# Low parts of the gate and up weights written over their raw chunks, with the next load waiting for the multiplication

## The reference, cut to what matters

```python
fn = rms_norm(h, g_ffn_pre[i])
ff = (jax.nn.silu(fn @ w_ffn_gate[i]) * (fn @ w_ffn_up[i])) @ w_ffn_down[i]
h = h + rms_norm(ff, g_ffn_post[i])
```

```python
c_act = jax.nn.silu(c)
mod = jnp.dot(c_act, w_ada[l]) + b_ada[l]
```

## Time and profile before

| | |
|---|---|
| median of 3 runs | 3594.81 us (3594.74 to 3598.14) |
| the profiled execution's own time | 3603.56 us |
| its span, first to last instruction | 3602.0 us |
| TensorE matmuls, busy | 3317.0 us, 92% of the span |
| VectorE busy | 1967.7 us, 55% |
| ScalarE busy | 1221.4 us, 34% |
| gate and up stage | about 540.7 to 1044.4 us |
| down stage | about 1044.4 to 1284 us |

### The profile page before, as it was taken

The page is one execution under the profiler, slowest core; times in us unless marked ns, Lnnn a source line. Parts: engine busy times, 40 slices in busy tenths (PEclk is TensorE's granted clock), DMA queues, the critical chain, the costliest instruction groups (busy, mean ns, idle before and its releaser), DMA issues.

```text
span 3602.0 us, 42919 instructions
## 1 busy us (share of the span) xinstructions
PE 3317.0 (92%) x15906; PEld 2611.5 (73%) x15906; DVE 1967.7 (55%) x2283; ACT 1221.4 (34%) x1263; POOL 823.4 (23%) x535
## 2 busy tenths in 40 slices
PE   7998779999999979789877799999999899999996
PEld 6874338888888844434556799888888688888885
DVE  4233457788865535550256579555555455555555
ACT  1122024444434420100242333455555343443431
POOL 2000000000000000000001478887888600100010
PEclk9999889999999989889988899999999899999998
DMA  7433547777755566579224256666666666666663
GB/s 257 141 123 111 187 152 272 273 278 279 277 191 191 198 234 247 219 273 358 75 84 163 94 179 178 211 216 214 210 212 216 181 248 235 244 240 242 238 246 116
DMA packets 194539, 747.53 MB, mean 208 GB/s; under 512 B 53873, under 2 KB 53905, under 8 KB 124321
## 3 DMA queue, kind: packets, MB, share of 16 engines
q1 hardware_dynamic: 129696, 664.84, 51.8%
q0 software_dynamic: 55552, 64.91, 6.7%
q10 hardware_dynamic: 9216, 16.78, 1.3%
HBM read 710.62 MB, written 35.83 MB: 207 GB/s over the span
## 4 chain that ended last, share of the span: by engine, by line
PE 69%; POOL 16%; DVE 8%; issue 4%; DMA 2%; ACT 2%; POOLq 0%; ACTq 0%; DVEq 0%; SPq 0%
POOL weight_dram L2107 15%; PE bank L435 15%; PE bank L581 10%; PE bank L582 10%; PE bank L583 10%; PE bank L587 9%; PE bank L419 7%; PE bank L588 5%; DMA weight_dram<-misc 1%; PE bank L372 1%; PE bank L850 1%; PE bank L484 1%; DVE aux L1916 0%; POOL part_lo L2087 0%; DMA misc<-in_w_ada 0%
## 5 line engine op out<-in xcount | busy, mean ns | idle before, releaser
L1880 DVE TENSOR_TENSOR part_lo<-ring,part_hi 128x2048 fp32r<-128x2048 f32 x248 | 568.0, 2293 | 406.5 <-ACT part_hi L1343 386.9
L1343 ACT ACTIVATE part_hi<-ring 128x2048 fp32r<-128x2048 f32 x252 | 482.8, 1916 | 550.9 <-PE bank L583 293.9
L2107 POOL DMA_INDIRECT weight_dram<-misc x256 | 571.1, 2231 | 101.6 <-issue 95.2
L587 PE MATMUL bank<-h_both,part_hi 128*128 128x512 f32 x1664 | 579.6, 392 | 8.1 <-DVE part_lo L1880 8.1
L435 PE MATMUL bank<-ring,xT 128*128 128x512 f32 (+1 forms) x1216 | 510.7, 581 | 8.0 <-DVE xT L1543 6.3
L587 PE MATMUL bank<-h_both,ffn_hi 128*128 128x512 f32 x1408 | 493.7, 397 | 4.8 <-DVE ffn_lo L1643 4.8
L588 PE MATMUL bank<-h_both,part_lo 128*128 128x256 f32 x1664 | 467.1, 281 | 0.0
L435 PEld LDWEIGHTS bank<-ring,xT 128*128 128x128 f32 x1216 | 226.9, 192 | 291.7 <-issue 289.9
L581 PE MATMUL bank<-part_hi,coef_hi 128*128 128x512 f32 x1024 | 399.7, 390 | 17.6 <-DVE part_lo L1880 17.6
L582 PE MATMUL bank<-part_lo,coef_hi 128*128 128x512 f32 x1024 | 399.4, 390 | 0.0
L583 PE MATMUL bank<-part_hi,coef_lo 128*128 128x512 f32 x1024 | 399.3, 390 | 0.0
(11 more groups left out here) (315 smaller groups left out, 4415.4 us busy)
## 6 DMA issues: line engine op xcount, KB each, us to landing
ring<-in_u_table SPq DMA_DIRECT2D x128, 1024.0 KB, 4.9
ring<-in_v_table SPq DMA_DIRECT2D x128, 1024.0 KB, 4.8
ring<-in_stream SPq DMA_DIRECT2D x114, 1024.0 KB, 6.3
misc<-in_w_ada SPq DMA_DIRECT2D x192, 512.0 KB, 5.7
ring<-in_gateup SPq DMA_DIRECT2D x88, 1024.0 KB, 4.9
ring<-in_down SPq DMA_DIRECT2D x44, 1024.0 KB, 4.8
ring<-in_wo_pq SPq DMA_DIRECT2D x32, 1024.0 KB, 4.8
weight_dram<-conv_tmp POOLq DMA_DIRECT2D x1, 16384.0 KB
```

The source lines that it names most:

```text
L587: nc.tensor.matmul(out[:, 0:2 * S], hi, x_pair, start=start, stop=False)
L1343: a.activation(part_hi[j % PARTS], raw[j % RAW], ACT.Copy).then_inc(sem("hi_ready"), 1)
L1880: v.tensor_tensor(part_lo[j % PARTS], raw[j % RAW], part_hi[j % PARTS].bitcast(F32), ALU.subtract).then_inc(sem("lo_ready"), 1)
L2107: g_.indirect_dma_start(out=places, out_offset=bass.IndirectOffsetOnAxis(ap=gstage[:, t, k:k + 1], axis=0), in_=wstage[:, t, k:k + 1], in_ ...
```

## The change: what it does

The low part of a gate or up chunk is written over the raw chunk (`down_lo`, four places), and the two places in `nat` are no longer used. VectorE's subtraction needs no wait for TensorE any more, and it is done one chunk earlier in VectorE's order (c + 3 in place of c + 2), so three are done ahead of the first round. The place of a raw chunk is now free only when TensorE has multiplied it, so SyncE's wait ahead of the chunk four later is on `multiplied`, and so is the wait of the first four chunks of down.

```diff
@@ -220,7 +220,6 @@
 
         ffn_raw = [ring[:, i * CH:(i + 1) * CH] for i in range(RAW)]
         ffn_hi = [rounded(f"ffn_hi{i}", "ring", (RAW + i) * CH, CH)[:, :] for i in range(PARTS)]
-        ffn_lo = [rounded(f"ffn_lo{i}", "nat", i * CH, CH)[:, :] for i in range(2)]
         down_lo = [rounded(f"down_lo{i}", "ring", i * CH, CH)[:, :] for i in range(RAW)]
         hid_parts = [rounded(f"hid_parts{i}", "misc", i * 8 * S, 8 * S)[:, :].rearrange("p (a k s) -> p a k s", a=2, k=4)
                      for i in range(2)]
@@ -708,7 +707,7 @@
                 for j in range(8):
                     if j < loads:
 
-                        sp_.wait_ge(sem("lo_ready"), j + 1 + 8 * it)
+                        sp_.wait_ge(multiplied, PLAN["gateup"]["chunk"] + j + 1 + 8 * it)
                         src = io["gateup"][RAW + j + 8 * it] if isinstance(it, int) else \
                             io["gateup"][bass.ds(RAW + j + 8 * it, 1)].rearrange("n p c -> (n p) c")
                         sp_.dma_start(ffn_raw[j % RAW], src).then_inc(raw_loaded[j % RAW], 16)
@@ -721,10 +720,7 @@
 
             for m in range(DOWN):
 
-                if m < RAW:
-                    sp_.wait_ge(sem("lo_ready"), SPLIT_DOWN - RAW + m + 1)
-                else:
-                    sp_.wait_ge(multiplied, gu_end + m - RAW + 1)
+                sp_.wait_ge(multiplied, gu_end + m - RAW + 1)
                 sp_.dma_start(ffn_raw[m % RAW], io["down"][m]).then_inc(raw_loaded[m % RAW], 16)
 
             down_end = PLAN["pproj"]["chunk"]
@@ -866,7 +862,7 @@
                     wait_bank(pe, "gateup", j, it, 8)
                     for k in range(KD):
                         ks = slice(k * P, (k + 1) * P)
-                        m = paired_products(out_bank("gateup", j), ffn_hi[j % PARTS][:, ks], ffn_lo[j % 2][:, ks],
+                        m = paired_products(out_bank("gateup", j), ffn_hi[j % PARTS][:, ks], down_lo[j % RAW][:, ks],
                                             h3_hi[:, k, :], h3_pair(k), k == 0, k == KD - 1)
                     m.then_inc(multiplied, 1)
 
@@ -1638,18 +1634,16 @@
 
             def ffn_lower(j, it=0, first=False):
                 v.wait_ge(sem("hi_ready"), j + 1 + 8 * it)
-                if not first:
-                    wait_multiplied(v, "gateup", j - 2, it, 8)
-                v.tensor_tensor(ffn_lo[j % 2], ffn_raw[j % RAW], ffn_hi[j % PARTS].bitcast(F32), ALU.subtract)\
+                v.tensor_tensor(down_lo[j % RAW], ffn_raw[j % RAW], ffn_hi[j % PARTS].bitcast(F32), ALU.subtract)\
                     .then_inc(sem("lo_ready"), 1)
 
             def gateup_round(it, first=False, last=False):
                 for c in range(8):
                     summed(c, it)
-                    if not (last and c >= 6):
-                        ffn_lower(2 + c, it)
+                    if not (last and c >= 5):
+                        ffn_lower(3 + c, it)
                     else:
-                        down_lower(c - 6)
+                        down_lower(c - 5)
                     if c % 2:
                         hidden(c // 2, it)
                     if last and c == 5:
@@ -1675,11 +1669,12 @@
 
             ffn_lower(0, first=True)
             ffn_lower(1, first=True)
+            ffn_lower(2, first=True)
             gateup_round(0, first=True)
             with steps.loop(KF // 4 - 2, 4) as it:
                 gateup_round(it + 1)
             gateup_round(KF // 4 - 1, last=True)
-            for m in range(2, DOWN):
+            for m in range(3, DOWN):
                 down_lower(m)
                 if m % 2 and 2 <= (m + 1) // 2 < 2 * HID_Q:
                     hidden_lo((m + 1) // 2)
```

## The result

The changed kernel takes 3644.5 us (median of 4 runs, 3635.1 to 3647.4) against 3595.9 us before (4 runs): a ratio of 1.0128, 95% interval 1.0113 to 1.0144; the medians are 48.6 us apart. The forecast was 3633 us, with a range of 3617 to 3655. Measured again later, with 4 runs and 13 of before, it was 3644.0 against 3600.1: ratio 1.0114 (1.0097 to 1.0131), medians 43.9 us apart. The profiled execution took 3643.98 us, its span is 3642.4 us, 40.4 more than before. The sum had given 3641.9 for it.

The account below looks back on a forecast made before the run. TensorE alone was taken to bound gate, up and down. Ten stops at ada_sum (+26.3 us) and clock drops (+12), all else 0, gave 3594.8 + 38.3 = 3633 us, range 3617 to 3655.

Parts of the forecast that it names:

- TensorE alone sets the pace: Gate, up and down: TensorE is busy throughout at clock 1.00, so shortening VectorE's or ScalarE's work gains nothing.
- Subtractions: cost 0: VectorE, gate, up and down: 88 and 44 subtractions before and after, 2292 ns in place against 2288 ns.
- the 5.6 us that the chain of chunk j + 4 had in hand: Gate and up: that chunk's subtraction ends near E(j) + 11 and is due at E(j) + 16.6, E being a chunk's end.
- The block behind the wait: SyncE's w_ada block leaves about 8 us later, so TensorE stops 2.63 us at ada_sum, ten times: +26.3 us.
- The clock: After the ada_sum stops TensorE's clock drops, 1.5 us for eight of the ten: +12 us.
- the pause of 2.44 us: Earlier TensorE pause, 2235.05 to 2237.50, followed by 3.41 us at clock 0.51; a loss of 1.4 us.
- by the Trainium skill the forecast would have been 3621 us: Rival: ten stops at ada_sum with the clock kept, +26.3 us alone; chance 0.17.
- The raw chunk later: Gate and up: raw chunks load only after multiplication, covered by the three chunks still in the ring; cost 0.
- Start and change of stage: Three subtractions before round one fit in VectorE's idle time; down's first four loads keep some 4 us in hand; cost 0.
- No change: Rival: later loads and modulation steps stay hidden, chain to ada_sum within 5.44 us, time 3595 us; chance 0.07.
- chunks late as well: Rival: raw chunks land over 5.6 us later, TensorE waits for low parts throughout, from some 3680 us up; chance 0.05.
- The range: Whole kernel: 3617 to 3655 us, within 3594.8 + 22 to 3594.8 + 62 by the bounds of landing and clock.

Follow-up runs that it names:

- The two versions without stops: Changed kernel with ada_sum between chunks 1 and 2: 3599.5 us; the same plus the w_ada block issued ahead of the raw-chunk wait: 3600.1 us.
- the shift undone: Changed kernel with the subtraction back at chunk c + 2 in VectorE's order, low parts still over the raw chunks: 3656.3 us, ratio 1.0150.
- the second profile: Profile of the changed kernel run again with no edit, beside the kernel before: 3644.0 us.
- the filled pause: Changed kernel with ten unread matmuls of 512 columns ahead of each ada_sum in ten rounds: 3633.0 us, ratio 1.0097.
- the waits alone: Kernel before with only SyncE's waits moved to the multiplication; low parts stay in nat, VectorE keeps its order: 3657.2 us, ratio 1.0157.
- block-first repair: Changed kernel with SyncE issuing the w_ada block ahead of its wait for the raw chunk: 3607.7 us, ratio 1.0027.
- run 24: Not a run number: in "the block-first run 24 and 41" it counts that run's chunks at 5.55 us; the run is the block-first repair, 3607.7 us.

## Why the prediction was right, step by step

- **TensorE alone sets the pace, so nothing can be gained.** Right. The two versions without stops give ratios of 1.0002 and 0.9998.
- **Subtractions: cost 0.** Right for their length: 2291 ns in place. What the step left out is what the earlier subtraction saves, some 12 us by the run with the shift undone. It was in the forecast only as the 5.6 us that the chain of chunk j + 4 had in hand; with c + 2 that margin would have been about nothing.
- **The block behind the wait: +26.3 us for ten stops.** Right, in mechanism, place and count. Measured 28.3 in ten. One differs: the first lasted 4.6 us, because a block of that round landed 7.7 us after its issue, outside the span of 5.5 to 6.7 in the earlier trace rows. The other nine are 2.5 to 3.1. The blocks issued from 586 to 596 us:

```profile
DMA to landing us min/median/max: 5.8/6.7/7.7
```

- **The clock: +12 us, as 1.5 for eight stops.** Right by its sum, off in its count, and there luck had a part: the forecast had eight drops of one length, the profile has them at six stops, one twice as long, and the second profile at seven. Measured about 10 us by the filled pause, 11 by the stretches. The row that decided between the ends was the pause of 2.44 us. The Trainium skill (TensorE: Matmul & The Clock Gate, section Why this matters for your kernels) warns only of longer pauses; here four of eight pauses of 2.5 to 2.7 us in the changed kernel were followed by the lower clock (and the two longer ones, 4.6 and 3.1), and with the waits alone all ten, of 2.5 to 3.0. In the second profile a pause of 3.27 us, longer than the Trainium skill's limit of about 3, was followed by no drop. The measurement decides: by the Trainium skill the forecast would have been 3621 us, below what was measured.
- **The raw chunk later: cost 0.** Right in the changed kernel. Not right as a general statement: with the stops gone by the block-first repair it held VectorE up by 0.85 us in the chunk shown.
- **Start and change of stage: 0.** Right: the wait at the start is 4.8 us as before, and no wait at down's first chunks.
- **No change, and chunks late as well.** Neither came. The chain was 8.1 us, not 5.44, and no product waited for a low part in the rounds.

- **The range.** Its lower end is worked out from +22 us, while the lowest of the sum's own terms is 25, with no drop of the clock; the 3 us between have no source. The result does not hang on it.

What the sum lacks is a term. The medians moved by 44 to 49 us, the sum said 38.3, and the profiled stage grew by 43.4. Stops (28.3) and clock (10 to 11) make 39. The other 4 to 5 us agree with a slower pace of TensorE, described in the last section; the forecast put that at nothing. The first medians are another 5 us apart; the later ones do not show that, and the first four runs of the changed kernel span 12 us.

## What to carry to other kernels

When a wait is moved on an in-order queue, follow what stands behind it before what it guards: by the forecast's working the raw chunk had 5.6 us in hand, while the small block behind it, at the end of a round, had none. Look for the consumer that another engine needs at a fixed place, here one matmul of a column of ones; moving it by one chunk was worth the whole loss. And price a short stop of TensorE above its length: ten stops, 28.3 us in all, made the stage 43.4 us longer, of which 10 to 11 were the clock.

## What the runs showed that was not expected

**Pauses of one length do not all lower the clock.** Pauses of like length were followed by a drop in one round and not in the next. In the changed kernel's first profile it was every second round from 650.2 on, in its second one seven rounds without such a pattern; with the waits alone it was every round, with the shift undone nine of ten. In these last two the rounds took some 51 us, in the changed kernel 49 to 51. Whether the length of the round decides was not tried. A forecast can give the price of one drop from rows, but the count only as a range: the same kernel had six and seven.

**TensorE has two paces for the same chunk.** SyncE's issues follow TensorE chunk by chunk and show them, both at clock 1.00, in the changed kernel:

```profile
729.30 0.33 SPq L713 DMA_DIRECT2D ring<-in_gateup  x1
...
734.96 0.33 SPq L713 DMA_DIRECT2D ring<-in_gateup  x1
...
740.61 0.33 SPq L713 DMA_DIRECT2D ring<-in_gateup  x1
```

```profile
768.29 0.33 SPq L713 DMA_DIRECT2D ring<-in_gateup  x1
...
773.84 0.33 SPq L713 DMA_DIRECT2D ring<-in_gateup  x1
...
779.38 0.33 SPq L713 DMA_DIRECT2D ring<-in_gateup  x1
```

It is 5.65 us in one round and 5.55 in the next, and the pace changes only at `ada_sum`. Taking chunks 2 to 7 of each round by the starts of their matmuls, the kernel before has 53 chunks at 5.55 and 12 at 5.65, and the two versions without stops are alike (50 and 14, 55 and 10). The changed kernel has 23 and 42, its second profile 6 and 59, the block-first run 24 and 41, the filled one 12 and 53. Kernels in which VectorE releases `ada_sum` late have more of the slow rounds, at 0.8 us a round. By these counts it is the rest of the sum, some 3 to 5 us, and 3 of the 7.6 us of the block-first run. That the late release is the cause is not shown: within the block-first run rounds behind an `ada_sum` without a wait were slow too, and some behind a wait of 0.2 to 0.3 us were not. What sets the pace at that point was not tried and stays open.
